# Experts of a routed MoE in units of one expert with 96 slots, in place of units of two experts with 64 slots each

## What is computed

```python
def hier_moe(h, p):                       # t: 640 tokens x 1024
    g_sel = argmax(t @ w_gr + b_gr)       # one of 4 groups
    e_in = (t @ w_er + b_er)[group g_sel] # its 8 experts
    top_v, top_i = lax.top_k(e_in, 2)     # two experts of that group
    top_w = softmax(top_v) * softmax(g_logit)[g_sel]
    a, u = t @ w1[e], t @ w3[e]           # 1024 -> 256, each of 32 experts
    y = (silu(a) * u * combine) @ w2[e]   # 256 -> 1024
    return sum over the token's two experts
x = x + g2 * hier_moe(rmsnorm(x) * (1 + sc2) + sh2)
```

## Time and profile before

| | |
|---|---|
| median of 3 runs | 1125.84 us |
| the profiled execution | 1126.69 us |
| its span in the trace | 1124.9 us |
| PE busy / mean granted clock | 90% / 0.954 |
| first expert row gathered (T of unit 0 begins) | 849.15 us |
| last projection but one ends | 1106.6 us |

### The profile page before, as it was taken

The page is one execution under the profiler, slowest core; times in us unless marked ns, Lnnn a source line. Parts: engine busy times, 40 slices in busy tenths (PEclk is TensorE's granted clock), DMA queues, the critical chain, the costliest instruction groups (busy, mean ns, idle before and its releaser), DMA issues.

```text
span 1124.9 us, 10780 instructions
## 1 busy us (share of the span) xinstructions
PE 1012.5 (90%) x4164; PEld 569.1 (51%) x4164; DVE 388.3 (35%) x845; ACT 225.1 (20%) x444; POOL 166.4 (15%) x160
## 2 busy tenths in 40 slices
PE   3899998999799989999999999989967997878775
PEld 1455554665455547777777777745543332323221
DVE  3213332135753422322323333226672322222122
ACT  3212630014244421101101011002110221111011
POOL 0000000010340013213223122100011111111111
PEclk9899999999989989999999999999977999999898
DMA  9635344200000144311312213083169999999993
GB/s 375 281 103 209 150 150 173 80 1 7 1 1 1 42 165 159 103 47 47 103 47 62 89 47 97 7 328 139 43 254 381 355 396 398 400 427 401 404 409 92
DMA packets 34003, 196.12 MB, mean 174 GB/s; under 512 B 7264, under 2 KB 11040, under 8 KB 22816
## 3 DMA queue, kind: packets, MB, share of 16 engines
q1 hardware_dynamic: 29040, 184.40, 41.7%
q0 software_dynamic: 4768, 10.50, 3.8%
q10 hardware_dynamic: 144, 0.52, 0.1%
HBM read 188.13 MB, written 14.09 MB: 180 GB/s over the span
## 4 chain that ended last, share of the span: by engine, by line
PE 85%; DMA 5%; issue 5%; DVE 3%; ACT 1%; POOL 0%; POOLq 0%; SPq 0%; DVEq 0%; ACTq 0%
PE psum L950 21%; PE psum L1131 11%; PE psum L685 8%; PE psum L967 8%; PE psum L1003 6%; PE psum L1147 5%; PE psum L801 3%; PE psum L887 3%; DMA r_w<-in_w_ada 2%; PE psum L686 2%; PE psum L901 2%; PE psum L694 2%; PE psum L911 2%; PE psum L1124 2%; DMA r_w<-h_scratch,tab 2%
## 5 line engine op out<-in xcount | busy, mean ns | idle before, releaser
L950 PE MATMUL psum<-r_h,r_w 128*128 128x320 f32 x512 | 143.3, 433 | 1.7 <-DVE r_d L1813 1.7
L2237 POOL TENSOR_TENSOR r_w<-r_w 128x512 f32<-128x512 f32 x64 | 80.6, 1271 | 316.0 <-PE psum L950 239.9
L950 PEld LDWEIGHTS psum<-r_h,r_w 128*128 128x128 f32 x512 | 97.2, 190 | 42.4 <-DVE r_d L1813 2.0
L950 PE MATMUL psum<-r_ys,r_w 128*128 128x320 f32 x384 | 108.6, 432 | 0.0
L685 PE MATMUL psum<-r_h,r_w 128*128 128x512 f32 x192 | 101.5, 611 | 1.5 <-DVE r_h L1576 1.5
L950 PEld LDWEIGHTS psum<-r_ys,r_w 128*128 128x128 f32 x384 | 73.0, 190 | 30.4
L1403 ACT ACTIVATE r_bv<-r_bv 128x320 f32<-128x320 f32 x64 | 30.1, 470 | 273.2 <-DVE r_bv L1860 273.2
L1003 PE MATMUL psum<-r_w,r_bv 128*128 128x512 f32 x160 | 72.3, 597 | 3.3 <-DVE r_bv L1855 3.3
L686 PEld LDWEIGHTS psum<-r_h,r_w 128*128 128x128 f32 x192 | 37.2, 194 | 47.5 <-issue 47.5
L2248 POOL DMA_INDIRECT out_y<-r_bv,tab x17 | 26.8, 1576 | 210.0 <-DVE r_bv L2088 189.2
L967 PE MATMUL psum<-r_ys,r_w 128*128 128x320 f32 x192 | 55.6, 432 | 0.0
(11 more groups left out here) (378 smaller groups left out, 1629.3 us busy)
## 6 DMA issues: line engine op xcount, KB each, us to landing
r_a<-in_w_ada SPq DMA_DIRECT2D x8, 2048.0 KB, 8.0
r_w<-in_w_gate SPq DMA_DIRECT2D x32, 512.0 KB, 4.7
r_a<-in_w_e SPq DMA_DIRECT2D x6, 2048.0 KB, 32.6
r_c<-in_w_e SPq DMA_DIRECT2D x6, 2048.0 KB, 32.5
r_w<-in_w_e SPq DMA_DIRECT2D x6, 2048.0 KB, 33.6
r_ys<-in_w_e SPq DMA_DIRECT2D x5, 2048.0 KB, 34.2
r_bv<-in_w_e SPq DMA_DIRECT2D x5, 2048.0 KB, 34.2
r_h<-in_w_e SPq DMA_DIRECT2D x5, 2048.0 KB
```

The source lines that it names most:

```text
L950: ins = mm(gate_bank(u, n), w[:, k, :], x[:, k, :], start=(k == 0), stop=(k == HK - 1))
L2237: g.tensor_tensor(w_mix[n], x, y, op).then_inc(s_wm, 1)
```

## The change

A unit is now one expert with `CAP` = 96 places; there are 32 units, no unit for overflow, and 32 loads of weights. The experts come in the same order as before (0, 8, 16, 24, 1, 9, ...). The table has 32 columns instead of 16; `weights` no longer adds the one-hots of a pair and keeps its columns for two tiles instead of five. The gather, the transposes, the copies and the scatter of a unit have 96 rows or columns instead of 128. The places of an expert are laid out over the partitions by another permutation (`places_of`). The sixth buffer and the order of the loads are kept; each load of a first part now has a wait of its own. `n_x` counts dynamic chunks from 96 upwards.

```diff
+CAP = 96
 C = 64
-EXTRA = PAIRS // 2
-EXPERT = [NE8 * (2 * (v // 2 % 2) + v % 2) + v // 4 for v in range(NE)]
-UNITS_E = [(EXPERT[2 * p], EXPERT[2 * p + 1]) for p in range(PAIRS)]
-UNITS_E.insert(EXTRA, (None,))
-LAST = len(UNITS_E) - 1
+LAST = NE - 1
+EXPERT = [NE8 * (u % NG) + u // NG for u in range(NE)]
-H_SLOT = (1, 3)
+H_SLOT = (3, 1)
...
-            AFTER = [[i + NBUF for i in AT[u] if i + NBUF < len(STREAM)] for u in range(LAST + 1)]
-            for u in range(LAST + 1):
-                if u == 2:
+            for u in range(LAST - NBUF + 1):
+                if u == 4:
...
+                sp.wait_ge(s_A, u + 1)
+                load_w13(u + NBUF)
+                if u == LAST - NBUF - 1:
+                    continue
+
+                for x in range(max(u - (2 if u == LAST - NBUF else 1), 0), u):
+                    sp.wait_ge(s_Y, x + 1)
+                    load_w2(x + NBUF)
...
-            def hidden(slot, halves, ks=range(KD)):
+            def hidden(slot, w, xT, n, ks=range(KD)):
 
                 for k in ks:
-                    for lo, w, xT in halves:
-                        ins = mm(psum[lo:lo + C, slot, 0:2 * FE], xT[:, k, :], w[:, k * 2 * FE:(k + 1) * 2 * FE],
-                                 start=(k == 0), stop=(k == KD - 1))
+                    ins = mm(psum[0:n, slot, 0:2 * FE], xT[:, k, 0:n], w[:, k * 2 * FE:(k + 1) * 2 * FE],
+                             start=(k == 0), stop=(k == KD - 1))
                 return ins
...
-                        for lo, homes, hid in halves:
-                            w = homes[f] if len(homes) == 2 else homes[0][:, f * D:(f + 1) * D]
-                            ins = mm(psum[lo:lo + C, 2, n * 512:(n + 1) * 512], hid[:, f, :],
-                                     w[:, n * 512:(n + 1) * 512], start=(f == 0), stop=(f == 1))
+                        w = homes[f] if len(homes) == 2 else homes[0][:, f * D:(f + 1) * D]
+                        ins = mm(psum[0:n, 2, h * 512:(h + 1) * 512], hid[:, f, :], w[:, h * 512:(h + 1) * 512],
+                                 start=(f == 0), stop=(f == 1))
...
+            def unit_T(u):
+                pe.wait_ge(xg_loaded[u % 2], 16 * (u // 2 + 1))
+                rows_T(xg[:, u % 2, :], CAP).then_inc(s_xT, 1)
...
-                step(v.tensor_tensor(r("hot").rearrange("p (i g e) -> p i g e", i=2, e=NE8), pairs[:, :, :, 0, :],
-                                     pairs[:, :, :, 1, :], ALU.add))
...
-                step(v.tensor_tensor(col_hot[:, :, t], spread(r3("hot", PAIRS), 3, 3),
-                                     spread(info2[:, :, t, :], 2, PAIRS), ALU.mult))
+                if t >= 2:
+                    dve.wait_ge(s_tabf, t - 1)
+                step(v.tensor_tensor(col_hot[:, t % 2], spread(m4[:, :, t, :], 3, 3), spread(info2[:, :, t, :], 2, NE), ALU.mult))
...
-                scatter(y_sb[0:n, u % 2, :], tab[0:n, TAB_COL[u], 0:1], y_stored[u % 2])
+                scatter(y_sb[0:CAP, u % 2, :], tab[0:CAP, EXPERT[u], 0:1], y_stored[u % 2])
...
-                gather(xg[0:n, u % 2, :], tab[0:n, TAB_COL[u], 0:1], xg_loaded[u % 2])
+                gather(xg[0:CAP, u % 2, :], tab[0:CAP, EXPERT[u], 0:1], xg_loaded[u % 2])
```

More of the change, by code:

```diff
@@ L584, in _, with load_w13, load_w2 @@
             sp.wait_ge(s_oTd, 4)
[L585 to L593, removed]
-                width = 2 * D // len(homes)
[L595 to L599, removed]
+            def load_w13(u):
+                sp.dma_start(wexp[u % NBUF][0], a["w_e"][EXPERT[u], :, 0:W13]).then_inc(w13_loaded[u % NBUF], 16)
+            def load_w2(u):
+                homes = wexp[u % NBUF][1:]
+                width = 2 * D // len(homes)
+                for n, home in enumerate(homes):
+                    sp.dma_start(home, a["w_e"][EXPERT[u], :, W13 + n * width:W13 + (n + 1) * width]) \
+                        .then_inc(w2_loaded[u % NBUF], 16)
             for e in range(2):
@@ L665, in _ @@
             overflow(sp, n_x, load_chunk)
-            sp.wait_ge(y_stored[0], 16 * (LAST // 2 + 1))
-            sp.wait_ge(y_stored[1], 16 * (LAST // 2))
+            for i in range(2):
+                sp.wait_ge(y_stored[i], 16 * (NE // 2))
             sp.wait_ge(s_x1d, 16 * TT)
@@ L1039, in table @@
                 for i in range(2):
-                    ins = mm(psum[:, 1, 512:512 + 3 * PAIRS], part_hot[t][:, i, :],
-                             col_hot[:, i, t].rearrange("p c k -> p (c k)"), start=(t == 0 and i == 0),
+                    ins = mm(psum[:, 1, 512:512 + 3 * NE], part_hot[t][:, i, :],
+                             col_hot[:, t % 2, i].rearrange("p c k -> p (c k)"), start=(t == 0 and i == 0),
                              stop=(t == TT - 1 and i == 1))
-                return ins
+                ins.then_inc(s_tabf, 1)
             pe.wait_ge(s_mdone, GATE_UNITS)
@@ L1133, in hidden, with hidden_T, project @@
                 return ins
-            def hidden_T(slot, x):
+            def hidden_T(slot, x, n):
                 for f in range(2):
-                    ins = flip(psum[:, slot, 512 + f * P:512 + (f + 1) * P], x[:, f * P:(f + 1) * P], ident)
+                    ins = flip(psum[:, slot, 512 + f * P:512 + f * P + n], x[0:n, f * P:(f + 1) * P], ident[0:n, 0:n])
                 return ins
-            def project(halves):
-                for n in range(2):
+            def project(homes, hid, n):
+                for h in range(2):
@@ L1155, in hidden_of @@
             def hidden_of(u):
-                for i in AT[u]:
-                    pe.wait_ge(w13_loaded[i % NBUF], 16 * (i // NBUF + 1))
+                pe.wait_ge(w13_loaded[u % NBUF], 16 * (u // NBUF + 1))
                 pe.wait_ge(s_xTd, u + 1)
-                halves = [(lo, wexp[i % NBUF][0], xgT[u % 2][:, :, lo:lo + C]) for lo, i in zip((0, C), AT[u])]
-                hidden(H_SLOT[u % 2], halves, range(0, KD // 2))
+                hidden(H_SLOT[u % 2], wexp[u % NBUF][0], xgT[u % 2], CAP, range(0, KD // 2))
@@ L1161, in hidden_of @@
                 if u:
[L1162 to L1166, removed]
+                    gate_T(u - 1)
+                hidden(H_SLOT[u % 2], wexp[u % NBUF][0], xgT[u % 2], CAP, range(KD // 2, KD)).then_inc(s_A, 1)
+            unit_T(0)
+            hidden_of(0)
+            unit_T(1)
             pe.wait_ge(s_cntd, 2)
-            hidden_of(0)
@@ L1179, in _ @@
                     pe.wait_ge(s_xTd, u + 2)
-                    pair_T(u + 2)
+                    unit_T(u + 2)
                 if u == LAST:
-                    pe.wait_ge(s_hid, u + 1)
-                    hidden_T(H_SLOT[u % 2], gate_e[:, u % 2, :]).then_inc(s_hf, 1)
-                for i in AT[u]:
-                    n = len(wexp[i % NBUF]) - 1
-                    pe.wait_ge(w2_loaded[i % NBUF], 16 * n * (i // NBUF + 1))
+                    gate_T(u)
+                homes = wexp[u % NBUF][1:]
+                pe.wait_ge(w2_loaded[u % NBUF], 16 * len(homes) * (u // NBUF + 1))
                 if u:
@@ L1189, in _ @@
                 pe.wait_ge(s_hT, u + 1)
-                project([(lo, wexp[i % NBUF][1:], hT[:, u % 2, :, lo:lo + C]) for lo, i in zip((0, C), AT[u])]) \
-                    .then_inc(s_Y, 1)
+                project(homes, hT[:, u % 2], CAP).then_inc(s_Y, 1)
                 if u != LAST - 1:
@@ L1487, in _ @@
                 for n in range(2):
-                    A(slot_g2[n], g2_row[:, 0, n * 512:(n + 1) * 512], ACT.Copy,
-                      scale=pair_w[:, TAB_COL[p], 0:1]).then_inc(s_gl, 1)
+                    A(slot_g2[n][0:CAP], g2_row[0:CAP, 0, n * 512:(n + 1) * 512], ACT.Copy,
+                      scale=slot_w[0:CAP, EXPERT[p], 0:1]).then_inc(s_gl, 1)
                 if p != LAST - 1:
@@ L2024, in _ @@
             dve.wait_ge(s_cnt, 1)
[L2025 to L2027 removed]
+            v.tensor_copy(r("pre"), psum[:, 1, 0:TT * NE]).then_inc(s_cntd, 1)
+            v.tensor_scalar(r("n"), psum[:, 1, TT * NE:(TT + 1) * NE], -float(CAP), None, ALU.add).then_inc(s_cntd, 1)
             dve.wait_ge(s_cntd, 2)
[L2029 removed]
+            step(v.scalar_tensor_tensor(out=over9, in0=spread(xio[:, 0:9], 1, NE), scalar=float(C),
                                         in1=spread(r("n"), 2, 9), op0=ALU.mult, op1=ALU.is_lt))
@@ L2249, in scatter @@
                                         bounds_check=NT - 1, oob_is_err=False, compute_op=ALU.add).then_inc(done, 16)
-            def rows_of(u):
-                return C if u == EXTRA else P
             def put_rows(u):
```

136 lines of the change are left out of this document (53 added, 83 removed).

## The result

The changed kernel takes 1228.74 us in the median of 4 runs (1226.69 to 1230.54), against 1125.4 us before (1124.9 to 1126.04): ratio 1.091, 95% interval 1.089 to 1.093. It is 103 us slower. The forecast was 125 us slower, and the measured time lies 13 us under the low end of the range. The direction and what bounds the kernel were as forecast; the length of a turn was not, and the range was too narrow to hold it.

A forecast was written before the change was run, and what follows sets the result against it. DMA bound before, TensorE after the change: unit 2's hidden matmuls at 877.1 us, 30 turns of 11.84 (354.3) and an end of 18.3 give span 1249.7; plus 1.79 outside, less 0.85, 1250.6 us; range 1242 to 1262.

The forecast's parts named there:

- What bounds the kernel: Before, DMA: 15.7 us of transfer a pair against 12.0 on PE; changed, each expert pays the pair's matmul price on TensorE.
- DMA still the bound: Rival: matmuls of two 96-wide units run beside each other, under 7.9 us of PE a unit; 1118 us, faster; chance 0.04.
- Tiling Modes: Skill's rule on PE column tiles: two tiles at 64 columns, one above, up to 2x; a 96-column unit takes the whole array.
- The turn: One expert's hidden matmuls, transposes and projection on PE: 11.84 us, between 11.65 and 12.00.
- the middle: In a turn's transposes: 0.90 us for eight and 0.34 for two, between time following width (0.77, 0.28) and not (1.03, 0.37).
- The other rule weighed: Transposes on PE: a transpose lasts about 275 ns, mostly access latency; narrowing saves nothing, the sum would be 4.8 us more.
- The sum: Unit 2's hidden matmuls at 877.1 us, 30 turns of 11.84 (354.3), end of 18.3: span 1249.7 us.
- The wait for the fifth gather: Before, unit 4's transposes waited 2.39 us for their gather; 4.1 us left out of the sum, kept as a bound.
- The end: From the last projection but one to the end of the span: 18.3 us kept, 1.9 us held as a possible gain.
- Gathers, loads, table: Gathers cost zero, landing within 15.1 us; loads zero, issued 59 us ahead; table zero, with 1 us either way.
- DMA share: Sign, from 870 to 1230 us: DMA engines' share near 0.66 at about 265 GB/s.
- The other signs: PE at 98% or more and clock 1.00 from 870 to 1230 us; 96-wide hidden matmuls every 0.43 us; 32 loads.

The follow-up runs named there:

- one-half experiment: Both experts of a pair write the same 64 PSUM partitions, one after the other, against the kernel before; 1249.13 us, ratio 1.110.

## Why the prediction was right, and where it was wrong

**What bounds the kernel: right.** The reading that a unit with one expert takes as long as a pair gave the direction, and it is shown by the one-half experiment (11.14 us an expert with 17 units) and, in a smaller dose, by the one that keeps the hidden matmuls apart (+53 us). The rival "DMA still the bound" is out: a turn takes 11.14 us, not under 7.9. The rule of the Trainium skill that the prediction took from TensorEngine Tiling (Array Packing), section Tiling Modes, holds here: units with 64 columns ran in twos, and hidden matmuls with 96 follow each other in single file, 8 records in 3.43 us.

**The turn: wrong by 0.70 us, and this is the step that failed.** "No row shows a transpose of 96, and I take the middle: 0.90 and 0.34", with "Hidden: 3.44 + 3.58 us, unchanged" and "Projection: 3.58, unchanged". All four numbers came from rows that stand next to matmuls with 64 columns. I took 3.58 as the price of a piece and 1.03 as an upper bound that could only shrink to 3/4. In each of them sat a passage of 0.14 to 0.16 us, which the change removes: four of them, 0.59 us a turn. The rest, 0.10, is the width of the transposes, 0.26 us less against the middle's 0.16. Both ends of my range for the turn (11.65 and 12.00) contained the passages, so the range could not hold the truth: with 30 turns at 11.14 us, the sum would have been 1229.6. There were rows that could have told: the first half of each turn, behind the projection, takes 3.44 and the second, behind transposes, 3.58, and I read past the difference; and 0.37 for 2 transposes with 1.03 for 8 already give the passage of 0.15 (the table above). The Trainium skill names it too, TensorEngine Tiling (Array Packing), Key Properties: changing the tiling mode drains the engine. The traces agree, at 0.15 us a change. The other rule weighed, the one that the prediction drew from the Trainium skill, TensorE: Matmul & The Clock Gate, Part 4: PE-mode transpose, that narrowing a transpose saves nothing, is contradicted for transposes in a row: 8 take 0.87 us with 128 columns and 0.66 with 96.

**The sum, term by term, for the profiled executions.** Forecast span 1249.7, trace 1224.9. 30 turns x 0.70 us are -21.0. The hidden matmuls of unit 2 begin at 870.38 instead of 877.1: -6.7, of which 3.9 already stand at the first transposes (845.29 against 849.15) and come from before the experts. They are luck, not the change: the output projection begins at 737.66 us here and at 743.87 in the trace of before, and at 743.91 in the trace of the changed kernel with places in plain order. Of the other 2.8, 1.4 are the first unit's hidden matmuls, which ran slower than later ones in both kernels, the granted clock having fallen to 0.5 over the waits ahead of them (16 record times at full clock are 6.87 us). The chain of before, then that of the changed kernel:

```profile
852.38 10.05 PE psum L1131 x32
```

```profile
847.89 8.62 PE psum L1117 x16
```

The other 1.4 are the shorter copy (0.82 us for 1.03), transposes and passages, for which the forecast had only 0.5. The wait for the fifth gather, which I left out, is there: 26.43 us from 870.38 to the turn at 896.81 where two turns are 22.28, +4.2. The end is 17.0 instead of 18.3 us, with a last projection of 3.66 instead of 5.37: -1.3. Together -24.8; the three terms behind the turn come to -3.8, so the miss is the turn's. The median then lies 2.05 us above the profiled execution where I had taken it 0.85 below, which gives the 22 us between 1250.6 and 1228.7.

**Gathers, loads, table: right.** 30 of the 32 gathers cost nothing. The first is waited for as before; the fifth was late because POOL's first scatter begins 5.4 us after its data are there and the gather behind it takes 11.2 us to land; I had argued that fewer loads in the queue would mend it, and they did not. The first parts of the loads land in 8 to 10 us in the median instead of 33 to 39 (849 us to the end).

**DMA share: partly wrong, without effect.** I expected 0.66 at 265 GB/s from 870 us on. From 870 to 1204 us it is 0.78 at 266 GB/s, and the rate agrees only because errors cancel. While loads run (942.60 to 1106.60 us) it is 0.89 at 310 GB/s: with turns of 11.14 us the weights alone are 282 GB/s, and gathers and scatters, which I had left out, move 4.87 MB in these 164 us, 30 GB/s. And the loads end at about 1160 us, some four turns before TensorE's last. The share is higher than the rate says: in that stretch SP's queue moved 45.89 MB of weights for 76.0% of the engines' time, before it was 58.76 MB for 84.9%; that is 15% more busy time a byte. Why is open. The other signs came as forecast: PE is busy for 331.88 of the 334 us at a clock of 0.99.

## What to carry to other kernels

Two matmuls with 64 stationary columns each that share the array halve TensorE's time for them, and a unit with 96 columns loses all of that at once: count TensorE's time per unit of work before merging or widening units to save transfers. A busy figure does not tell what binds: PE at 81% or at 99.9% of the stage gave the same total within 0.3% as long as the transfers took 15.7 us a pair. And a piece's duration belongs to its neighbours as well: compare the same piece behind different predecessors before carrying its time into a new order.

## What the runs showed of the hardware that I had not expected

- A passage between matmuls with 64 stationary columns and full-array transposes costs 0.14 to 0.15 us; with it, a turn of one expert with 64 columns (11.50 us) is longer than one with 96 (11.14).
- Matmuls for the other 64 partitions start before earlier ones are done: with 8 records of one expert ahead of 8 of another in the program, the second begins with the fifth record of the first (912.24 us), and 4 ahead of 4 in the projection cost hardly more than alternating ones (3.63 us against 3.58).
- POOL's first scatter begins 5 to 7 us after its data are there in all ten traces, whatever the kernel (5.4 us with the change); the second follows its data within 1 us. Why is open.
- What lies ahead of the output projection, which neither the change nor an experiment touches, ends at different times: the projection begins between 737.66 and 744.46 us in the ten traces. The kernel before, 1124.9 to 1126.04 in its first runs, was 1121.6 to 1129.8 in the later ones. What can be told from no change with 3 or 4 runs is nearer to 0.4% (half of that spread) than to the 0.2% I had stated.
